# A decoder step's mixture of experts on one core: experts visited by row count, the fullest eleventh with its extra rows, the five lightest last on four 32-column strips

## The reference

```python
def hier_moe(n, w_group, b_group, w_router, b_router, w_gate, w_up, w_down):
    ...
    top_w, top_i = lax.top_k(jax.nn.softmax(e_logits, axis=-1), TOP_K_IN_GROUP)
    top_w = top_w / jnp.sum(top_w, axis=-1, keepdims=True) * g_gate
    ...
    for e in range(N_EXPERTS):
        h = jax.nn.silu(xf @ w_gate[e]) * (xf @ w_up[e])
        y = y + combine[:, e:e + 1] * (h @ w_down[e])
```

## Time and profile before

| | us |
|---|---|
| three runs | 1281.4, 1287.35, 1291.57 |
| median | 1287.35 |
| span of the profiled execution, first to last instruction | 1276.9 |

### The profile page before, as it was taken

How to read it: one execution, slowest core, us unless ns; L and a number is a source line. 1 busy time by engine, 2 the same in 40 slices (tenths; PEclk the granted TensorE clock), 3 DMA queues, 4 the chain that set the end, 5 groups by cost and what they waited for, 6 DMA issues and landing times.

```text
span 1276.9 us, 13642 instructions
## 1 busy us (share of the span) xinstructions
PE 1219.7 (96%) x5650; PEld 577.9 (45%) x5650; DVE 494.6 (39%) x965; ACT 187.0 (15%) x393; POOL 51.6 (4%) x67
## 2 busy tenths in 40 slices
PE   7999999999999988999998998999999999999996
PEld 4344443344444445777785763333333333333332
DVE  5000275199464563111115551333333333333335
ACT  2011233300221333000014220000000000000000
POOL 0002000000000022100000010000000000000000
PEclk9999999999999999999999998999999999999999
DMA  8836523355333377744455377999999999999962
GB/s 280 297 131 153 156 86 102 130 183 165 130 102 99 103 265 297 271 137 134 139 189 231 137 296 316 409 430 427 427 427 426 427 428 427 427 427 424 428 263 76
DMA packets 71083, 332.01 MB, mean 260 GB/s; under 512 B 13516, under 2 KB 17388, under 8 KB 54444
## 3 DMA queue, kind: packets, MB, share of 16 engines
q1 hardware_dynamic: 54576, 282.65, 56.7%
q0 software_dynamic: 8464, 41.42, 8.5%
q10 hardware_dynamic: 7980, 7.05, 2.2%
HBM read 320.61 MB, written 10.49 MB: 259 GB/s over the span
## 4 chain that ended last, share of the span: by engine, by line
PE 78%; DVE 8%; DMA 8%; ACT 3%; ACTq 1%; issue 1%; POOL 0%; DVEq 0%; SPq 0%
PE PS L669 19%; PE PS L1254 16%; PE PS L976 15%; PE PS L1311 8%; PE PS L1218 5%; PE PS L642 3%; DMA NC<-in_w_up 2%; DMA ring<-in_w_up 2%; DVE X L1875 2%; DVE top L1874 2%; PE PS L787 1%; PE PS L1300 1%; PE PS L1222 1%; DMA X<-in_cache_v,ids 1%; DVE NC L2237 1%
## 5 line engine op out<-in xcount | busy, mean ns | idle before, releaser
L669 PE MATMUL PS<-ring,NC 128*128 128x512 f32 x704 | 322.6, 603 | 1.6 <-issue 1.6
L669 PEld LDWEIGHTS PS<-ring,NC 128*128 128x128 f32 x704 | 129.3, 192 | 154.4 <-issue 152.8
L976 PE MATMUL PS<-NC,ring 128*128 128x288 f32 x768 | 189.9, 407 | 1.6 <-issue 0.5
L1254 PE MATMUL PS<-ring,NC 128*64 128x512 f32 x768 | 178.4, 603 | 4.1 <-DMA ring<-in_w_up 2.7
L976 PEld LDWEIGHTS PS<-NC,ring 128*128 128x128 f32 x768 | 144.6, 190 | 42.4 <-issue 2.9
L2205 DVE TENSOR_TENSOR X<-X,PS 128x1024 f32<-128x1024 f32 x64 | 78.2, 1221 | 148.5 <-PE PS L1218 148.5
L1254 PEld LDWEIGHTS PS<-ring,NC 128*64 128x64 f32 x768 | 51.4, 137 | 123.6 <-issue 122.0
L1311 PE MATMUL PS<-ring,NC 128*64 128x512 f32 x384 | 87.9, 612 | 0.5 <-ACT NC L1756 0.5
L1754 ACT ACTIVATE NC<-PS,small 64x512 f32<-64x512 f32 x16 | 10.9, 680 | 437.7 <-PE PS L1254 437.7
L1218 PE MATMUL PS<-XNN,NC 64*128 64x512 f32 x256 | 72.3, 641 | 0.3 <-DVE XNN L2247 0.3
L1254 PE MATMUL PS<-XNN,NC 128*64 128x512 f32 x128 | 59.0, 599 | 1.2 <-DMA NC<-in_w_up 1.2
(11 more groups left out here) (412 smaller groups left out, 1072.4 us busy)
## 6 DMA issues: line engine op xcount, KB each, us to landing
ring<-in_w_gate SPq DMA_DIRECT2D x24, 2048.0 KB, 18.3
ring<-in_w_up SPq DMA_DIRECT2D x24, 2048.0 KB, 21.8
ring<-in_w_down SPq DMA_DIRECT2D x24, 2048.0 KB, 20.1
ring<-in_w_in SPq DMA_DIRECT2D x36, 1024.0 KB, 5.1
ring<-in_w_out SPq DMA_DIRECT2D x16, 1024.0 KB, 5.1
XNN<-in_w_gate SPq DMA_DIRECT2D x8, 2048.0 KB, 18.9
NC<-in_w_up SPq DMA_DIRECT2D x8, 2048.0 KB, 21.8
XNN<-in_w_down SPq DMA_DIRECT2D x4, 2048.0 KB, 21.5
```

The source lines that it names most:

```text
L669: last = mm(acc(n, t)[:, 0:width], lhs[:, kt, t * 128:(t + 1) * 128], slot(m)[:, k, 0:width], start=kt == 0, stop=kt == KT - 1)
L976: last = mm(PS[:, j, 0:NT], slot(m)[:, k, 128 * j:128 * j + 128], src[:, kt, :], start=kt == 0, stop=kt == width * 4 - 1)
L1254: last = mm(PS[64 * half:64 * half + 64, 2, :], XT[:, 4 * (kt // 4 % 2) + kt % 4, kt // 8, :], w, start=kt == 0, stop=kt == KT - 1)
```

## The change

Experts are visited by row count. Expert 0 is still first, since its weights come before the counts are known. Places 1 to 9 take the next fullest of the others after the star, place 10 (`PSTAR`) the star with its 64 and its 32 extra rows, and places 11 to 15 the five lightest, with a limit of 32 rows each.

- `star_gate_up`: in each half of D eight steps of full products, then eight steps of the strip products of the extra rows (bank 3), from the same weights; `star_down` in the same manner. The pass behind the last expert, `star_table` and `star_combine` are gone.
- `light_gate_up`, `light_down`: one light expert on four strips (L1275, L1327 of the new kernel), 32 rows stationary.
- Blocks: 11 of 64 rows; then the star's extra rows and expert 11 share block 11, experts 12 and 13 block 12, 14 and 15 block 13: 14 gathers. A block of two is combined once, behind its second expert. Its rows reach `ysb` by two copies of 32 x 512 on VectorE and two on ScalarE per expert.
- Rows of the odd of these blocks are laid in `mkT` (`XT2`).
- An empty slot points past the end of `nsc` (`EMPTY`), and the gather has a bounds check that skips such rows.
- The order of the experts is computed on VectorE after the first table, and SyncE reads it behind the third `hot_ready`.
- The overflow code moves ahead of the last light expert's down products. The last six combining steps use 64 stationary rows, and the six stores take two pieces of 512 columns a row.

```diff
-STAR = 32
-NBLK = NEXP + 1 + NOVF
+STRIP = 32
+NLIGHT = 5
+PSTAR = NEXP - 1 - NLIGHT
+NBK = PSTAR + 1 + (NLIGHT + 1) // 2
+NBLK = NBK + NOVF
+EMPTY = 512
...
-    put("tok", (p + 128 * np.arange(3)[None, :]).astype(np.float32))
+    put("tok", (p + 128 * np.arange(3)[None, :] - EMPTY).astype(np.float32))
...
-    put("half", (p >= 64).astype(np.float32))
+    put("half", ((p >= 64) + 2 * EMPTY).astype(np.float32))
...
                 if e == 1:
-                    sp.wait_ge(S("hot_ready"), 2)
+                    sp.wait_ge(S("hot_ready"), 3)
...
-                                             bass.IndirectOffsetOnAxis(ap=tabS[:, b:b + 1], axis=0)).then_inc(S(done), 16)
-            for e in range(NEXP + 1):
-                if e >= 2:
-                    pool.wait_ge(S("xt_ready"), e - 1)
-                block_rows(e, e % 2, f"xg_in{e % 2}")
+                                             bass.IndirectOffsetOnAxis(ap=tabS[:, b:b + 1], axis=0),
+                                             bounds_check=2 * NT - 1, oob_is_err=False).then_inc(S(done), 16)
+            for b in range(NBK):
+                if b >= 2:
+                    pool.wait_ge(S("xt_ready"), b - 1)
+                block_rows(b, b % 2, f"xg_in{b % 2}")
...
+            def strip_products(x, sub, bank, weights, kt):
+
+                for c in range(4):
+                    last = mm(PS[32 * c:32 * c + 32, bank, 0:256], x[:, kt % 8, kt // 8, STRIP * sub:STRIP * sub + STRIP],
+                              weights[c // 2][:, kt % 8, 256 * (c % 2):256 * (c % 2) + 256], start=kt == 0, stop=kt == KT - 1)
+                    yield last
...
+            def light_gate_up(x, sub, landed, between):
 
                 for kt in range(KT):
-                    if kt % 3 == 2 and kt < 12:
+                    if kt % 3 == 2:
                         between(kt // 3)
...
+                    if kt % 8 == 0:
+                        weights = lots_of(landed, kt // 8)
+                    for c, last in enumerate(strip_products(x, sub, 2, weights, kt)):
+                        if kt % 8 == 7 and c % 2:
+                            last.then_inc(S("moe_free"), 1)
...
-                if e == 0:
-                    pe.wait_ge(S("route_ready"), 1)
-                    star_table().then_inc(S("tab_sum"), 1)
...
-            own(V.tensor_reduce(star_max, fill[:, 1:16], AXX, ALU.max))
-            own(TS(is_star[:, 1:16], fill[:, 1:16], star_max, None, ALU.is_equal))
-            own(TS(limit, is_star, float(STAR), float(CAP), ALU.mult, ALU.add))
+            each = [128, 15, 15]
+            own(TT(fuller, bc(fill[:, 1:16], 1, each), bc(fill[:, 1:16], 2, each), ALU.is_gt))
+            own(V.tensor_reduce(rnk[:, 1:16], fuller, AXX, ALU.add))
+            own(TS(s32[:, 1:16], rnk[:, 1:16], 0.0, float(STRIP), ALU.is_equal, ALU.mult))
+            own(TS(l32[:, 1:16], rnk[:, 1:16], float(PSTAR), float(CAP - STRIP), ALU.is_ge, ALU.mult))
+            own(STT(limit, s32, float(CAP), l32, ALU.add, ALU.subtract))
...
+            own(TT(who, bc(at_place, 1, [1, 16, 16]), bc(cc("iota_e", 1), 2, [1, 16, 16]), ALU.is_equal))
+            own(TT(who, who, bc(cc("iota_e", 1), 1, [1, 16, 16]), ALU.mult))
+            own(V.tensor_reduce(at_place, who, AXX, ALU.add))
+            V.tensor_copy(ids_order, at_place).then_inc(S("hot_ready"), 1)
```

More of the change, by code:

```diff
@@ L414, in decode_step @@
         NLOT = NEXP * NL
+        HELD = [(NLOT - 2 + i) % NRING for i in range(2)]
+        SPARE = [i for i in range(NRING) if i not in HELD][:NL]
+        FREED = NLOT + NRING - 2
+        NCOMB_IN = NCOMB * (NBK - 1)
         r_at = [0]
@@ L1322, in landed, with light_down, lots_at @@
+            def light_down(bank, landed, done):
+                for q in range(2):
+                    w = landed(4 + q).rearrange("p (f n) -> p f n", f=2)
+                    for f in range(2 * q, 2 * q + 2):
+                        last = strip_down(bank, w, f)
+                    done(last, q)
+            def lots_at(p):
                 def landed(i):
[L1323 removed]
+                    lot = NL * p + i
                     pe.wait_ge(S(f"moe_in{lot % NRING}"), 16 * (lot // NRING + 1))
@@ new lines, in _ @@
+            keep_clock(5)
+            block_rows_t(0)
+            for p in range(PSTAR):
+                pe.wait_ge(S("xt_laid"), p + 1)
+                gate_up(lots_at(p), lambda s: combine_step(p - 1, s) if p and s < 4 else None)
+                block_rows_t(p + 1)
+                pe.wait_ge(S("hidden"), p + 1)
+                hidden_t().then_inc(S("ht_ready"), 1)
+                if p:
+                    combine_step(p - 1, 4)
+                if p + 1 == PSTAR:
+                    block_rows_t(PSTAR + 1)
+                pe.wait_ge(S("ht_laid"), p + 1)
+                if p:
+                    pe.wait_ge(S("y_out_psum"), p)
+                down(lots_at(p))
@@ new lines, in _ @@
+            pe.wait_ge(S("y_strips"), 2 * (NLIGHT + 1))
+            for n, (t, x) in enumerate(LAST[:4]):
+                last_combine(t, x, 2 * n)
+            pe.wait_ge(S("y_ready"), 1)
+            for half in range(2):
+                rows = slice(64 * half, 64 * half + 64)
+                for x in range(2):
+                    last = mm(PS[32 * x:32 * x + 32, half, :], slot_w[rows, (NBK - 1) % 2, T:NT],
+                              ysb[rows, (NBK - 1) % 2, 512 * x:512 * x + 512], start=True, stop=True)
@@ new lines, in _ @@
+            strip_rows(PSTAR + 1, 0, 1)
+            for p in range(PSTAR + 1, NEXP):
+                b, sub = block_of(p), sub_of(p)
+                before = PSTAR if p == PSTAR + 1 else b - 1 if not sub else None
+                if before is not None:
+                    combined(before, range(4))
+                if sub:
+                    block_weights(b)
+                dve.wait_ge(S("silu"), p + 2)
+                STT(hid[64:128, 0:256], PS[64:128, 2, 0:256], strips[64:128, sub, b - PSTAR - 1:b - PSTAR], sg[64:128, 0:256],
+                    ALU.mult, ALU.mult).then_inc(S("hidden"), 1)
+                if sub and b + 1 < NBK:
+                    next_rows(b + 1, (XT, XT2)[(b + 1 - PSTAR) % 2])
+                if before is not None:
+                    combined(before, (4,))
+                if p < NEXP - 1:
+                    dve.wait_ge(S("moe_free"), NL * p + NRING + NL)
+                    strip_rows(b, sub, 4 + sub)
```

417 lines of the change are left out of this document (247 added, 170 removed).

## The result

The changed kernel takes 1252.86 us, the median of 4 runs (1249.68 to 1254.33), where the kernel before took 1285.05 (1281.4 to 1291.57): a ratio of 0.974, interval 0.9706 to 0.9775, -32.2 us. The forecast was 1246.5 with a range of 1238 to 1266: the direction and the range hold, the size of the gain (40.9) was too large by a quarter.

The account below looks back on a forecast made before the run. It took the weight transfers, slower than TensorE by 1.5 us an expert, plus the work behind the last landing as the bound. 1219.0 + 4.0 + 11.3 + 0.7 + 1.0 = 1236.0, -40.9 us; 1287.35 - 40.9 = 1246.5, range 1238 to 1266.

Parts of the forecast that it names:

- the signs that the prediction named: Whole kernel: landing at 1217 to 1221, light-expert waits of 3 to 6 us, no 48-record group, 328 MB, 15 to 20 us behind.
- "The first block": the start: Ahead of expert 0's gate-up: TensorE starts when its clock-keeping ends, -0.7 us, bounds 2 earlier to 4 later.
- "The first block": star table and clock: Around expert 0's down: removing the star table saves 2.93 us, and a better clock 1.5 (0 to 2.9).
- Last landing: 1232.7 - 5.1 - 8.6: End of the weight stream: first-block gain 5.1 and gather bytes 8.6 us, both taken in full, give 1219.0.
- the DMA share never leaves 1.00: Weight stream before the change: DMA queue full from lot 14's issue at 811.55 to 1232.7 us, at 425 GB/s.
- I expect no hole in the stream worth over 1 us.: At the fullest (star) block: some 10 us of queue backlog covers the longer block, so the weight stream does not run dry.
- Behind the last landing.: End of kernel: 4.0 us to finish products (1.9 to 8.5), then 11.3, plus 0.7 for copies and 1.0 for clock.
- 10.45 us ... around the span in both kernels.: Outside the profiled span: the three-run median lies 10.45 us above it, taken as lying around the span in both kernels.
- (a): Gathers: skipped rows move all the same, +4.9 us, giving 1251, still faster; chance 0.18.
- (b): Light experts: low clock makes TensorE the bound, 162 us instead of 87, time 1287, no change; chance 0.08.
- (c): Fullest block: clock already low there, 79 us instead of 40.4, time 1327, slower; chance 0.03.
- (d): Light experts: one has over 32 rows, so an overflow block runs, +47, time 1294, within 1%; chance 0.01.

Follow-up runs that it names:

- e6: e2 plus 8 added full-width products in each of experts 11, 12 and 13; median 1254.42 us, 0.9766 of the kernel before.
- e3: Changed kernel with 24 three-column products (48 records) put back behind expert 0's gate-up; median 1253.89 us, 0.9772 of the kernel before.
- e4: Changed kernel with the edits of both e1 and e2; median 1255.13 us, 0.9761 of the kernel before.
- e5: e2 plus 10 and 12 dummy 512-column products ahead of the halves of the last expert's gate-up; median 1258.73 us, ratio 0.9808.
- e9: e8 plus 53 padding products of 64 columns at place 12; median 1249.27 us, 0.9746 of the kernel before.
- e10: e3 plus 40 small products of 64 columns among the light experts; median 1255.2 us, 0.9787 of the kernel before.
- e1: Changed kernel with empty gather slots fetching row 0 again instead of being skipped; median 1252.65 us, 0.9733 of the kernel before.
- e2: Changed kernel with VectorE laying block 10's rows before the fifth combining additions at place 9; median 1248.95 us, ratio 0.9719.
- e7: Kernel before with one edit, empty gather slots skipped; median 1279.76 us of 10 runs, 0.9966 of the kernel before.
- e0: Changed kernel run again unedited, for scatter; median 1253.18 us, 0.9746 of the kernel before.
- e8: e2 plus 5 and 6 dummy 512-column products ahead of the halves of the last expert's gate-up; median 1251.63 us, ratio 0.9763.

## Why the prediction was right or wrong

**Right in direction and, in the main, in its mechanism.** TensorE waits for weights in the last experts (the two largest waits of TensorE after 811 us):

```profile
engine line waited for: us in total, times, longest us
PE PS L1275 <- DMA ring<-in_w_up: 22.7, 4, 6.5
PE PS L1222 <- DVE NC L2365: 3.9, 1, 3.9
```

The landing sets the end, the work behind it shrank to the down products and the last combining, and the bytes are 327.85 MB where 328 was written. Of the signs that the prediction named, the waits (3.8 to 6.5 us, beside one of 1.1), the bytes, the missing 48 records and the 15 to 20 us behind the landing came; a landing at 1217 to 1221 did not: 455.6 us behind the first gate-up is 1226.3 in before's times. The time itself came nearer (6.4 us off) than the gain (8.7 off), since the forecast started from a median of three, 1287.35, that a fourth run brought down to 1285.05; that part is luck. e6 confirms that the light experts' saved TensorE time buys nothing but the end.

**"The first block": the start.** Forecast -0.7, measured 29.9 us from the ranking products to the first gate-up against 29.6: +0.3, so 1.0 us of the miss. The prediction had it right that TensorE's clock-keeping would end last, and not the gather. After, the issue of the first gather (us to landing), the clock-keeping, and lot 7, which waits for the gather:

```profile
NC<-nsc,tabS POOLq DMA_INDIRECT x1, 3.5
...
767.75 6.90 PE L1211 MATMUL PS<-cst 128*128 128x512 f32 x10
...
769.67 0.34 SPq L534 DMA_DIRECT2D NC<-in_w_up  x1
```

The gather, ahead of lot 6 now, took 3.5 us where it had taken 8.98. But the clock-keeping begins 20.5 us behind the ranking products where it began at 18.7, 1.7 later and not 1.0, and takes 6.90 us for 6.25. The 1.0 is also within what the same code scatters by: from the ranking products to the first gate-up it took 28.4 us in five runs (e3, e4, e5, e9, e10), 29.9 to 30.0 in five, 31.2 in e1 and 33.6 in e2.

**"The first block": star table and clock.** 2.9 + 1.5 were written; lot 14 is issued 33.6 us behind the first gate-up (810.76 - 777.18) instead of 40.9 (811.55 - 770.7), -7.3. The clock's part (9.94 to 7.09, so 2.9) was at its upper bound, and 1.6 are the first gate-up's, which was in no term. I had the size too small, but what failed is the next step: this time was added in full to what the bytes save ("Last landing: 1232.7 - 5.1 - 8.6"). The two overlap. When lot 14 comes earlier, lots 8 to 13 are still in the queue, and it mostly waits behind them; what it gives is the gap that would be there otherwise. That gap is small: "the DMA share never leaves 1.00" from 811.55 us on was read from a mean, and before has 318 GB/s over 810 to 815, a loss of 1.3 us. From the first gate-up to the landing, before and e2:

```profile
770.72:1233.20 462.48, 455.94 (x2110) 157.91 (x2112) 162.58 (x158) 15.95 (x30) 13.05 (x14) 0.99 0.99 420
...
775.03:1227.30 452.27, 415.12 (x2564) 154.60 (x2564) 150.07 (x159) 21.70 (x43) 11.26 (x12) 0.96 0.99 420
```

Both run at 420 GB/s. So the 10.2 us between them are 4.3 MB less to move, and the whole of the smaller gathers is 4.2 MB. By e7 the gathers alone are worth 5.4 to 7.2 us, which leaves 3.0 to 4.8 for the first block; by the bytes they are worth nearly all of it. The runs do not settle how the 10.2 part, but the sum is measured: I had 4.4 (5.1 less the start's 0.7) and 8.6, which is 13.0, so 2.8 too much.

**"I expect no hole in the stream worth over 1 us."** This step failed too, and by more than the others. The hole cost 3.3 to 3.9 us of landing (455.6 and 456.2 against 452.3). The prediction named a DMA share under 0.95 around the fullest block as the sign of it, and the share is 0.93. It looked at the fullest block's own length (and had 40.4 for 44.2 us: TensorE waits 2.0 us around its hidden part, and the first half of its down takes 5.46 us where the second takes 3.65), but not at place 9, where two blocks are transposed in a row and the second waits on VectorE: 3.90 us, and 2.2 more in the products behind it. That the block before the fullest needs both sets is in the code. Start, overlap and hole: 1.0 + 2.8 + 3.3 = 7.1 us.

**"Behind the last landing."** Forecast 17.0, measured 19.4 (19.1 in e0). The down products end 6.1 us behind the landing (1238.95 - 1232.85), where 4 were taken within bounds of 1.9 and 8.5; from there to the end are 13.25 us where 13.0 were written. The term that was mis-sized is the clock, by 2.1: the strip gate-up takes 6.19 us instead of 3.66, the first half of the down 3.31 instead of 1.92. With before's end at 43.7 where the earlier trace rows were read as 44.2, this part gave 24.3 us for 27.2, 2.9 less. With the 7.1 above, this is the difference of 10.0 between -40.9 and the -30.9 that the stage shows from its ranking products to the end (535.8 to 504.9).

**"10.45 us ... around the span in both kernels."** Wrong: 1.8 us lie around the span. The rest was a profiled execution that was quicker than the median ahead of this stage. A difference that is added to a median doesn't hurt from this; the forecast time does only so far as the stretches upstream differ, and the medians (-32.2) agree with the stage (-30.9).

**The rivals.** (a), that skipped rows move, is refuted by the bytes of after against e1. Had it been so, e1 shows that the time would hardly have changed; the prediction gave it 4.9 us. (b) is there in a small part: the granted clock is 0.83 over the light experts, whose waits for weights show that TensorE isn't the bound there. The Trainium skill, "TensorE: Matmul & The Clock Gate", Part 1, holds that the throttled state is the default and activity releases it. The trace agrees: behind a wait of 3.83 us a strip gate-up takes 6.19 us, with 0.50 granted from 1225.2 to 1229.2. What the prediction made of it, five light experts near 1.2 GHz throughout, did not come: 0.83 is the mean of stretches at full and at half clock. (c) and (d) did not happen: the fullest block is 44.2 us long, not 79, and no overflow products run.

## What to carry to other kernels

When one stream of transfers ends a stage, bytes saved and an earlier start of one late transfer don't add up: ask at each place whether the queue is full, and give the gain once. Where a change makes one block longer, look also at the block before it, whose engine queues must prepare it: a producer that stands behind unrelated work (here additions of 2.4 us) opens a hole that costs about as much as its wait (3.3 to 3.9 us of landing for 3.90), and which is closed by an order of two lines. Read a queue's fullness from short stretches, since a mean of 1.00 over 421 us hid one of 5 us at 318 GB/s. Take differences from a fixed point inside the stage that changed, not from spans, when what runs ahead of it scatters by more than the effect.

## What the hardware showed that I had not expected

**A pause behind a jump that depends on where its target lies.** TensorE jumps over the overflow code ahead of the last down products. Between its last product ahead of that and the first behind it, with no engine waited for, stood 3.49 us (e3), 3.50 (e5) and 4.12 (e6), in e8 1.48 inside the down products, and in before some 0.6 to 1.2 between the two pieces of its down in the earlier trace rows. In after, e0, e1, e2 and e4 there is none, the wait being ScalarE's 0.5 to 0.6. Padding of 40 or 53 small products ahead, no other edit, removed it in both kernels where it was tried (e3 to e10, e8 to e9), and the page's instruction queue then shows one packet more:

```profile
q8 instruction: 48, 0.79, 0.3%
```

in after, and in e10:

```profile
q8 instruction: 49, 0.80, 0.3%
```

That TensorE waits there for its instructions to be brought is the reading that fits; the trace has no row of such a wait, and it was not shown otherwise. For a study it means that an edit anywhere ahead of a jump can move the end by 3 to 4 us, so a run with such a pause says nothing on small effects.

**Three-column products bring the clock down.** 48 records of 1.38 us in all, with no wait ahead of them, made the 7.09 us of down behind them 8.74 (e3, e10). A wait does it too: behind the 3.90 us at place 9 the down took 8.38.

**A skipped row moves nothing.** 14 blocks of 64 slots hold 576 pairs and 320 empty slots; at 8 KB each these are 2.62 MB, and that is what after moves less than e1 (330.47 - 327.85). So an empty slot costs no bytes at all with the bounds check.
